# A state-space stage rearranged to four PSUM banks, with the first two tile pairs of the gated projection accumulated inside it

## What is computed

```
u = h.reshape(B, L, 64 groups, 16)              # L = 512, 64 states in each group
bu = einsum('blgc,gpc->blgp', u, bb)            # complex input matrix
x  = associative_scan(a, bu)                    # complex diagonal recurrence over time
y  = einsum('blgp,gcp->blgc', x_re, c_re) - einsum('blgp,gcp->blgc', x_im, c_im)
y  = y + d_skip * u
g  = gelu(y)
ga, gb = split(g @ w_glu, 2)                    # w_glu is 1024 x 2048
out = ga * sigmoid(gb)
```

## Time and profile before

| | us |
|---|---|
| median of 3 runs | 2806.56 (2805.25 to 2806.91) |
| profiled execution, its own time | 2804.32 |
| its span, first to last instruction | 2802.5 |
| TensorE busy in it | 2686.7 |
| VectorE busy | 1348.4 |
| state-space stage and gated projection, first input product to last projection matmul | 2169.0 to 2378.5 |

### The profile page before, as it was taken

The page is one execution under the profiler, slowest core; times in us unless marked ns, Lnnn a source line. Parts: engine busy times, 40 slices in busy tenths (PEclk is TensorE's granted clock), DMA queues, the critical chain, the costliest instruction groups (busy, mean ns, idle before and its releaser), DMA issues. The chain is left out here.

```text
span 2802.5 us, 29209 instructions
## 1 busy us (share of the span) xinstructions
PE 2686.7 (96%) x11452; PEld 1966.3 (70%) x11452; DVE 1348.4 (48%) x2184; ACT 569.6 (20%) x1054; POOL 836.2 (30%) x694
## 2 busy tenths in 40 slices
PE   8999999999999999999999889999997589999999
PEld 7888885655545888887654546888644544888888
DVE  5544313146533554524498634555562942666521
ACT  2000002211201000002335532222203410222200
POOL 5444430000213544341000223443020822344432
PEclk9999999999999999999999999999998799999999
DMA  7455322211113555422122002223323212122221
GB/s 232 160 172 167 119 83 85 76 50 60 45 60 101 177 171 170 133 85 89 46 61 74 31 16 75 91 83 98 111 49 88 74 60 86 65 91 90 74 96 57
DMA packets 248404, 262.82 MB, mean 94 GB/s; under 512 B 31864, under 2 KB 232908, under 8 KB 248140
## 3 DMA queue, kind: packets, MB, share of 16 engines
q1 hardware_dynamic: 232620, 206.77, 23.6%
q10 hardware_dynamic: 15648, 54.18, 5.7%
HBM read 253.97 MB, written 6.29 MB: 93 GB/s over the span
## 5 line engine op out<-in xcount | busy, mean ns | idle before, releaser
L614 PE MATMUL ps<-hT,ring 128*128 128x256 f32 x2816 | 656.1, 381 | 2.9 <-ACT hT L1041 1.4
L614 PEld LDWEIGHTS ps<-hT,ring 128*128 128x128 f32 x2816 | 537.5, 191 | 79.2 <-issue 3.4
L614 PE MATMUL ps<-phase,ring 128*128 128x256 f32 x2112 | 498.4, 379 | 0.0
L542 POOL TENSOR_TENSOR ring<-ring 128x512 f32<-128x512 f32 (+1 forms) x124 | 158.7, 1280 | 1019.8 <-DMA ring<-in_ffn_w 519.7
L614 PEld LDWEIGHTS ps<-phase,ring 128*128 128x128 f32 x2112 | 400.5, 190 | 54.0
L670 PE MATMUL ps<-phase,ring 128*128 128x256 f32 x1848 | 400.6, 379 | 1.3 <-issue 1.3
L670 PEld LDWEIGHTS ps<-phase,ring 128*128 128x128 f32 x1848 | 350.7, 190 | 49.1 <-issue 1.7
L1142 PE MATMUL ps<-hT,ring 128*128 128x512 f32 x512 | 227.2, 601 | 3.1 <-ACT phase L1326 2.6
L1606 PE MATMUL ps<-hT,ring 128*128 128x512 f32 x448 | 195.8, 594 | 1.4 <-ACT hT L1041 0.9
L545 POOL TENSOR_TENSOR ring<-ring 128x512 f32<-128x512 f32 (+1 forms) x124 | 189.2, 1526 | 0.0
L696 DVE TENSOR_TENSOR act_t<-u,ps 128x256 f32<-128x256 f32 x176 | 73.3, 420 | 240.5 <-PE ps L614 240.2
(11 more groups left out here) (331 smaller groups left out, 2981.8 us busy)
## 6 DMA issues: line engine op xcount, KB each, us to landing
ring<-in_ffn_w SPq DMA_DIRECT2D x60, 1024.0 KB, 5.3
ring<-in_ffn_w_up SPq DMA_DIRECT2D x44, 1024.0 KB, 5.1
phase<-in_ada_w ACTq DMA_DIRECT2D x64, 512.0 KB, 4.4
ring<-in_w_in SPq DMA_DIRECT2D x19, 1024.0 KB, 5.3
sq<-in_ada_w ACTq DMA_DIRECT2D x32, 512.0 KB, 4.2
ring<-in_attn_w_in SPq DMA_DIRECT2D x14, 1024.0 KB, 5.1
ring<-in_ffn_w_down SPq DMA_DIRECT2D x8, 1408.0 KB, 6.5
ring<-in_ssm_w_glu SPq DMA_DIRECT2D x8, 1024.0 KB, 6.2
```

The costliest lines, as they stand in the source:

```text
L542: pool.tensor_tensor(s1, a21, a22, ALU.add).then_inc(combined, 1)
L614: mm = pe.matmul(ps[:, 4 * w + bank_of[name], 0:HALF], left[:, c], right[name](c), start=(opens and c == 0), stop=(c == KC // 2 - 1), skip ...
```

## The change

Input products of every unit now go to banks 0 and 1, and outputs alternate between banks 2 and 3. The input products of unit `c` wait for the rotation of unit `c - 1` (before: `c - 2`). The direct products of unit `d` move one iteration back, behind the input products of unit `d + 1`, with a semaphore of their own (`s_direct`); SP's reload of the stacked buffer for unit `c` waits for it, since it overwrites what unit `c - 2`'s direct products read. They wait for the gelu of unit `d - 2` because the output bank is shared with it. The freed banks 4 to 7 take tile pairs 0 and 1 of the projection, which are accumulated one chunk at a time inside the stage: 4 matmuls (two pairs, two halves) for chunk `c - 5` in iteration `c`. Behind the stage come chunks 5 and 6 of both pairs, the first 7 chunks of pair 2, then the last chunk of all three, then the other pairs, which rotate over all 8 banks.

```diff
--- before.py
+++ after.py
@@ -2365,6 +2365,7 @@
         s_stack = [sem(f"ssm_stacked{b}") for b in range(2)]
         s_yrow = [sem(f"ssm_y_stored{b}") for b in range(2)]
         s_back = [sem(f"ssm_y_returned{c}") for c in range(KC)]
+        s_direct = sem("ssm_direct_added")
         s_bu = sem("ssm_input")
         s_near = sem("ssm_near")
         s_frac = sem("ssm_frac")
@@ -2408,6 +2409,7 @@
                 sp.wait_ge(s_urow[c % 2], 16 * (c // 2 + 1))
                 if c >= 2:
                     sp.wait_ge(s_bu, 2 * (c - 1))
+                    sp.wait_ge(s_direct, 2 * (c - 1))
                 rows_of = u_dram[c].rearrange("(v j x) (i k) -> j i x v k", j=2, v=4, i=STRIDE)
                 for j in range(2):
                     for i in range(STRIDE):
@@ -2420,22 +2422,32 @@
             for c in range(KC - 4, KC):
                 back(c)
 
-        GLU_EARLY = 4
+        def glu_bank(p):
+
+            return (4 + 2 * p) % 8
+
+        def y_bank(c):
+
+            return 2 + c % 2
 
         def ssm_pe(pe):
-            def glu(p, chunks, halves=(0, 1)):
+            def glu(p, chunks):
 
                 b, j = p // 2, p % 2
-                for w in halves:
+                for w in range(2):
                     if j == 0 and chunks[0] == 0:
                         slot_wait(pe, n3 + 2 * b + w)
                     for c in chunks:
-                        if p == 0:
-                            pe.wait_ge(s_back[c], 128)
-                        mm = pe.matmul(ps[:, 2 * (p % 2) + w, :], wtile(n3 + 2 * b + w, c, KC, j * P, (j + 1) * P),
+                        mm = pe.matmul(ps[:, glu_bank(p) + w, :], wtile(n3 + 2 * b + w, c, KC, j * P, (j + 1) * P),
                                        hT[:, c, :], start=(c == 0), stop=(c == KC - 1))
                     if chunks[-1] == KC - 1:
                         mm.then_inc(tile_done, 1)
+
+            def glu_early(c):
+
+                pe.wait_ge(s_back[c], 128)
+                for p in range(2):
+                    glu(p, [c])
 
             def each():
 
@@ -2447,42 +2459,52 @@
             for c in range(SSM_UNITS + 2):
                 if c < SSM_UNITS:
                     pe.wait_ge(s_stack[c % 2], 128 * (c // 2 + 1))
-                    if c >= 2:
-                        pe.wait_ge(s_pre, 4 * (c - 2) + 4)
+                    if c >= 1:
+                        pe.wait_ge(s_pre, 4 * (c - 1) + 4)
                     for n in range(2):
                         for t, half, cols in each():
-                            pe.matmul(ps[half, 2 * (c % 2) + n, cols],
-                                      BT[n][half, 2 * c + t // 2, (t % 2) * HD:(t % 2 + 1) * HD],
-                                      stacked[half, c % 2, cols], start=True, stop=True)
-                    if c == 0:
+                            mm = pe.matmul(ps[half, n, cols],
+                                           BT[n][half, 2 * c + t // 2, (t % 2) * HD:(t % 2 + 1) * HD],
+                                           stacked[half, c % 2, cols], start=True, stop=True)
+                            if n == 1 and t == 3:
+                                mm.then_inc(s_bu, 1)
+                if 1 <= c <= SSM_UNITS:
+                    d = c - 1
+                    if d == 0:
                         pe.wait_ge(s_dir, 16 * 32)
-                    if c == 2:
-                        pe.wait_ge(h_ready, h_before(6) + KC)
-                    if c >= 4:
-                        pe.wait_ge(s_g, c - 3)
+                    if d >= 2:
+                        pe.wait_ge(s_g, d - 1)
                     for t, half, cols in each():
-                        mm = pe.matmul(ps[half, 4 + (c + 2) % 4, cols], direct[half, 2 * c + t // 2, t % 2, :],
-                                       stacked[half, c % 2, cols], start=(t == 0), stop=False, skip_group_check=True)
+                        mm = pe.matmul(ps[half, y_bank(d), cols], direct[half, 2 * d + t // 2, t % 2, :],
+                                       stacked[half, d % 2, cols], start=(t == 0), stop=False, skip_group_check=True)
                         if t == 3:
-                            mm.then_inc(s_bu, 1)
+                            mm.then_inc(s_direct, 1)
+                if c == 5:
+                    pe.wait_ge(h_ready, h_before(6) + KC)
+                if c >= 5:
+                    glu_early(c - 5)
                 if c >= 2:
                     v = c - 2
-                    if v >= SSM_UNITS - 2:
-                        pe.wait_ge(s_pre, 4 * SSM_UNITS)
-                        glu(0, range(GLU_EARLY), (v - (SSM_UNITS - 2),))
                     pe.wait_ge(s_postd, 3 * v + 3)
                     pe.wait_ge(s_postp, 3 * v + 3)
                     for n in range(2):
                         for t, half, cols in each():
-                            mm = pe.matmul(ps[half, 4 + (v + 2) % 4, cols], CA[n][half, 4 * v + t, 1:5, :],
+                            mm = pe.matmul(ps[half, y_bank(v), cols], CA[n][half, 4 * v + t, 1:5, :],
                                            state[v % 2][half, n, t, 0:NK], start=False, stop=(n == 1),
                                            skip_group_check=True)
                             if n == 1 and t == 3:
                                 mm.then_inc(s_y, 1)
-            glu(0, range(GLU_EARLY, KC))
-            for p in range(1, KC):
-                if p >= 2:
-                    pe.wait_ge(s_glu, p - 1)
+            glu_early(5)
+            glu_early(6)
+            glu(2, range(KC - 1))
+            pe.wait_ge(s_back[KC - 1], 128)
+            for p in range(3):
+                glu(p, [KC - 1])
+            for p in range(3, KC):
+                if p == 3:
+                    pe.wait_ge(s_g, SSM_UNITS)
+                if p >= 4:
+                    pe.wait_ge(s_glu, p - 3)
                 glu(p, range(KC))
 
         TURN = 6.283185
@@ -2532,7 +2554,7 @@
                 act.wait_ge(s_y, 2 * (c + 1))
                 if c >= 2:
                     act.wait_ge(s_yrow[c % 2], 16 * (c // 2))
-                act.activation(gelu_rows[c % 2][:, :], ps[:, 4 + (c + 2) % 4, :], ACT.Gelu_apprx_tanh).then_inc(s_g, 1)
+                act.activation(gelu_rows[c % 2][:, :], ps[:, y_bank(c), :], ACT.Gelu_apprx_tanh).then_inc(s_g, 1)
                 act.wait_ge(s_g, c + 1)
                 act.dma_start(y_dram[c], gelu_rows[c % 2][:, :]).then_inc(s_yrow[c % 2], 16)
 
@@ -2549,7 +2571,7 @@
                 act.wait_ge(tile_done, e3 + 2 * p + 2)
                 if p >= 2:
                     act.wait_ge(s_glu, p - 1)
-                act.activation(act_t[:, p % 2, :], ps[:, 2 * (p % 2) + 1, :], ACT.Sigmoid).then_inc(s_sig, 1)
+                act.activation(act_t[:, p % 2, :], ps[:, glu_bank(p) + 1, :], ACT.Sigmoid).then_inc(s_sig, 1)
                 if p >= 1:
                     square(act, 7, p - 1)
             square(act, 7, KC - 1)
@@ -2563,7 +2585,7 @@
                 if u >= 2:
                     dve.wait_ge(s_add, 2 * (u - 2) + 2)
                 for n, (source, tab) in enumerate(((0, cosT), (1, sinT), (1, cosT), (0, sinT))):
-                    dve.tensor_tensor(pre[:, 4 * b + n, :], ps[:, 2 * b + source, :], tab[u % 3], ALU.mult)\
+                    dve.tensor_tensor(pre[:, 4 * b + n, :], ps[:, source, :], tab[u % 3], ALU.mult)\
                         .then_inc(s_pre, 1)
 
             def scan(u):
@@ -2603,7 +2625,7 @@
                     rotate_back(u - 1)
             for p in range(KC):
                 dve.wait_ge(s_sig, p + 1)
-                dve.tensor_tensor(act_t[:, p % 2, :], ps[:, 2 * (p % 2), :], act_t[:, p % 2, :], ALU.mult)\
+                dve.tensor_tensor(act_t[:, p % 2, :], ps[:, glu_bank(p), :], act_t[:, p % 2, :], ALU.mult)\
                     .then_inc(s_glu, 1)
                 dve.wait_ge(s_glu, p + 1)
                 by_time = xT[:, p, :].rearrange("p (k r) -> p r k", r=STRIDE)
```

## The result

The changed kernel takes 2786.88 us (median of 4 runs, 2785.20 to 2789.86) against 2806.73 for the kernel before; the ratio is 0.9936, interval 0.9924 to 0.9948, that is 14.6 to 21.3 us less. 2790.5 was forecast, in a range of 2788.0 to 2797.5. Measured by the ratio from 2806.56, the figure that the forecast started from, it is 2788.6 (2785.2 to 2792.0), just inside the lower end.

A forecast was written before the change was run, and what follows sets the result against it. VectorE was taken to bound the stage and TensorE's queue of 117 projection matmuls the time behind it. Terms of -17.2 and +1.2 us summed to -16.0, from 2806.56 to 2790.5 us, range 2788.0 to 2797.5.

The forecast's parts named there:

- What bounds: VectorE sets the stage's pace, rotations 11.76 us apart; then TensorE's unbroken queue of 117 projection matmuls, 102.1 us.
- Term one: Behind the last state products: 108 projection matmuls instead of 120, last chunk's return hidden, cold start gone; -17.2 us.
- Term two: At unit 1, input products wait for unit 0's rotation; second rotation 0.6 to 2.3 us later, charged +1.2 us.
- The bursts at nothing: Four projection matmuls in each of iterations 5 to 9, 3.7 us each, fit TensorE's holes and cost nothing.
- rival 2: Cold bursts take 7.0 us and overrun their holes, last state products 2.8 us late; 2793.5 to 2795, chance 0.10.
- idle under 1 us ahead of state products in units 3 to 5: Sign to look for on TensorE in the stage: under 1 us of idle there if the forecast holds.
- Direct products and SP's loads: Direct products wait 2 us for a gelu; stacked loads wait for direct products, 4.5 us of slack left; nothing charged.
- rival 4: SP's queue becomes the loop, an older unit's return between stacked loads: 17.0 us a unit, net +10, 2817; chance 0.04.
- Weights: Projection's tail: reloads asked for at 2291.3 and 2292.1, landed by 2304.5, three microseconds before pair 4 needs them.
- Sum: Whole program: -17.2 + 1.2 = -16.0 us, median from 2806.56 to 2790.5.

The follow-up runs named there:

- tail_only: Kernel before with only the projection's tail reordered, so the last chunk is asked for behind more matmuls; stage 203.55 us, ratio 0.9978 to the kernel before.
- two_bursts: Changed kernel without the bursts of iterations 5 to 7, keeping those of 8 and 9; stage 202.13 us, ratio 0.9975 to the kernel before.
- banks_only: Changed kernel's banks and later direct products, but the projection scheduled as in the kernel before; stage 209.08 us, ratio 0.9999 to the kernel before.
- direct_last: Changed kernel with direct products behind the burst of four projection matmuls instead of ahead of it; stage 195.13 us, one run of 2788.38 us.
- no_cover: Changed kernel without pair 2's matmuls ahead of the last chunk; stage 193.41 us, ratio 0.9950 to the kernel before.
- after_again: Changed kernel run and profiled once more, unaltered; stage 194.12 us, ratio 0.9931 to the kernel before.

## Why the prediction was right

**What bounds.** Right: VectorE's pace in the stage, then TensorE's queue. Steady rotations stayed 11.74 to 11.78 us apart, and 10.1 at the last unit, in every kernel but the two that delayed the direct products.

**Term one, -17.2.** Measured -16.2 (109.91 to 93.67 us from the end of the last state products to the end of the stage). The count of matmuls and the 0.858 us held: 0.860 wherever the queue ran at the higher clock from its start. What was missed is a cold start of 0.8 us in the new queue; I had written that it goes. The term splits into 5.9 us from the order of the tail, measured by tail_only, and 12 x 0.860 = 10.3 from the bursts, which two_bursts bears out once the clock is set aside. That 22 matmuls of cover are needed was not claimed, and 8 are enough to within 1.0 us. For chunk 6 the working names two figures for how much earlier it started than the last one, 4.1 and 6.2 us, which can't both hold; nothing hangs on it, since the 216 records show no gap.

**Term two, +1.2.** The second rotation was late by 1.8 us, inside the 0.6 to 2.3 forecast, but "VectorE has no slack to give it back" was wrong: the third rotation was on time. The measured cost is 0, in banks_only too. That it is just 0 is not a law: with a second rotation only a little later, as in direct_last, the rest would have gone through.

**The bursts at nothing.** Right for the pace of VectorE. The last state products took 0.86 us longer, a price that I had put into rival 2 alone, but it isn't shown to be one of the bursts: no_cover has all five of them and the same hole, and took 1.97. Not the bursts were cold, but what followed the hole behind the last one. Rival 2's mechanism was weighed there with the Trainium skill ("TensorE: Matmul & The Clock Gate", section "Why this matters for your kernels"), which advises, for thin operands, to go through the whole contraction before the next wait for a DMA. It showed at a single burst, 4.82 us at 2222.65, where TensorE had waited for a gelu; four of five took the warm 3.70, and all five in after_again. The sign "idle under 1 us ahead of state products in units 3 to 5" failed for unit 4, with 1.48 us, at no cost.

**Direct products and SP's loads.** The wait on the gelu came out at 2.16 us, and the slack of the loads at 5.0 in direct_last, where I had 4.5. A loop through SP can bound the stage: with direct products behind the state products it takes the whole gain. It isn't the loop of rival 4, which had the return of an older unit in it; here the return issued from 2227.89 is done by 2231.6, 8 us before the next load is released, and the state products and the burst fill the loop. Rival 4's own loop was seen in no run.

**Weights.** No gap ahead of pair 4. The reloads were asked for at 2290.25, where 2291.3 was forecast.

**Sum.** -16.0 forecast; the stage gave -15.3 and -16.9 in two pairs of profiles. That it comes so close is in part luck: two errors, 1.2 too much cost at unit 1 and 1.7 too little for the clock, nearly cancelled. The runs' ratios, 0.9936 and 0.9931, lie at 18.0 and 19.4 us, 2.0 and 3.4 us more than forecast; their lower ends, 14.6 and 16.0 us, come close to the stage's figures. In the profiled executions the rest is ahead of the stage, where the profiles differ by up to 9 us between kernels with the same code there. Whether some 2 us of it belong to the change stays open.

## What to carry to other kernels

Where one engine sets the pace of a stage and another's queue follows it, count the holes of the second engine in the stage and move whole pieces of its later queue there: here each was worth its full 0.86 us, once the differences of the clock are set aside, as long as it fitted into the hole. Before building new buffers for that, try the order of the tail: asking for the last piece behind twenty matmuls instead of three gave more than a third of the gain with a few lines, and eight would hide all but 1 us of it. When a reader of a double buffer is moved later, compute the loop through the refill; here it had some 5 us left, and the next step of delay cost about as much as the change had won (15.9 us of the stage against 15.3).

## What was not expected of the hardware

The 8 scans behind VectorE's second rotation took 5.38 to 6.88 us, in the main the longer the earlier they began beside GpSimd's work, so that the third rotation started at 20.3 to 21.5 us wherever between 7.0 and 9.7 the second one had started.

The same hole of 1.99 us ahead of the last state products was followed by the lower clock in the kernel after, twice (2.83 and 2.73 us for the last state products), and by the higher one in no_cover, two_bursts and banks_only (1.97). A hole of this length may or may not cost 1.6 us; what decides it no run shows. With it filled, in two kernels with one profile each, it did not.
